# Attention B: the values of a pair of heads weighed on 64 output columns each, in plain float32

## The reference, cut to what matters

```python
def swa_mixer(h, w_in, b_in, sinks, w_out, b_out, rel_bias):
    ...
    kk, vv = with_prev(k), with_prev(v)
    logits = jnp.einsum('bnqkgd,bnskd->bnkgqs', q, kk).astype(jnp.float32) * (Dh ** -0.5)
    ...
    p = jax.nn.softmax(jnp.concatenate([logits, sink], axis=-1), axis=-1)[..., :-1]
    o = jnp.einsum('bnkgqs,bnskd->bnqkgd', p.astype(vv.dtype), vv)
    return o.reshape(B, T, N_HEADS * Dh) @ w_out + b_out
```

## Time and profile before

| | before |
|---|---|
| median of 3 runs | 1174.75 us (1174.5 to 1175.15) |
| profiled execution, device time | 1174.45 us |
| its span, first to last instruction | 1172.7 us |
| PE busy | 1153.3 us |
| PEld busy | 962.8 us |
| POOL busy | 610.4 us |
| DVE busy | 529.9 us |
| ACT busy | 458.0 us |
| granted TensorE clock, mean | 0.998 |

### The profile page before, as it was taken

The page is one execution under the profiler, slowest core; times in us unless marked ns, Lnnn a source line. Parts: engine busy times, 40 slices in busy tenths (PEclk is TensorE's granted clock), DMA queues, the critical chain, the costliest instruction groups (busy, mean ns, idle before and its releaser), DMA issues.

```text
span 1172.7 us, 16085 instructions
## 1 busy us (share of the span) xinstructions
PE 1153.3 (98%) x5666; PEld 962.8 (82%) x5666; DVE 529.9 (45%) x931; ACT 458.0 (39%) x854; POOL 610.4 (52%) x359
## 2 busy tenths in 40 slices
PE   7999999999999999999999999999999999999997
PEld 5778889888888888888888888888888888888887
DVE  5479967743543443441111376645444434420001
ACT  5343267754333223223222477643322332322333
POOL 5427667864454454444444587834445544534441
PEclk9999999999999999999999999999999999999999
DMA  7442311123323323323443332322333333232331
GB/s 241 151 136 72 126 37 46 46 72 108 104 76 107 107 77 102 107 75 106 142 129 102 102 86 57 66 70 74 108 107 89 89 107 99 68 90 88 94 98 72
DMA packets 181572, 112.46 MB, mean 96 GB/s; under 512 B 7340, under 2 KB 175591, under 8 KB 181528
## 3 DMA queue, kind: packets, MB, share of 16 engines
q1 hardware_dynamic: 180860, 110.71, 31.7%
q10 hardware_dynamic: 668, 1.19, 0.3%
HBM read 109.72 MB, written 8.45 MB: 101 GB/s over the span
## 4 chain that ended last, share of the span: by engine, by line
PE 93%; DVE 3%; issue 1%; ACT 1%; POOL 1%; DMA 1%; ACTq 0%; DVEq 0%
PE ps L607 29%; PE ps L609 29%; PE ps L608 29%; PE ps L616 1%; PE ps L842 1%; DVE work L1639 1%; PE ps L1021 1%; PE ps L816 1%; DMA x_tok<-in_x 1%; DVE work L1621 0%; PE ps L1024 0%; POOL w_lo L494 0%; POOL work L554 0%; PE ps L655 0%; DVE xs_lo L1524 0%
## 5 line engine op out<-in xcount | busy, mean ns | idle before, releaser
L494 POOL TENSOR_TENSOR w_lo<-raw,w_hi 128x1024 fp32r<-128x1024 f32 (+1 forms) x198 | 454.1, 2316 | 479.7 <-ACT w_hi L1147 471.1
L607 PE MATMUL ps<-xs_hi,w_hi 128*128 128x512 f32 (+3 forms) x1024 | 397.2, 388 | 4.0 <-POOL w_lo L494 1.6
L608 PE MATMUL ps<-xs_lo,w_hi 128*128 128x512 f32 (+3 forms) x1024 | 394.4, 385 | 0.0
L609 PE MATMUL ps<-xs_hi,w_lo 128*128 128x512 f32 (+3 forms) x1024 | 394.3, 385 | 0.0
L1147 ACT CAST w_hi<-raw 128x1024 fp32r<-128x1024 f32 (+1 forms) x194 | 177.1, 962 | 430.3 <-PE ps L609 430.3
L607 PEld LDWEIGHTS ps<-xs_hi,w_hi 128*128 128x128 f32 x1024 | 192.2, 188 | 47.4 <-issue 4.1
L608 PEld LDWEIGHTS ps<-xs_lo,w_hi 128*128 128x128 f32 x1024 | 192.3, 188 | 39.1 <-issue 1.0
L609 PEld LDWEIGHTS ps<-xs_hi,w_lo 128*128 128x128 f32 x1024 | 192.3, 188 | 38.5
L607 PE MATMUL ps<-act_hi,w_hi 128*128 128x512 f32 (+1 forms) x374 | 141.6, 379 | 0.0
L609 PE MATMUL ps<-act_hi,w_lo 128*128 128x512 f32 (+1 forms) x374 | 140.9, 377 | 0.0
L608 PE MATMUL ps<-act_lo,w_hi 128*128 128x512 f32 (+1 forms) x374 | 140.8, 377 | 0.0
(11 more groups left out here) (191 smaller groups left out, 1348.0 us busy)
## 6 DMA issues: line engine op xcount, KB each, us to landing
raw<-in_ffn_w_gate_up SPq DMA_DIRECT2D x88, 512.0 KB, 4.3
raw<-in_ffn_w_down SPq DMA_DIRECT2D x32, 384.0 KB, 3.4
raw<-in_a_w_in SPq DMA_DIRECT2D x20, 512.0 KB, 4.8
raw<-in_ffn_w_down SPq DMA_DIRECT2D x32, 320.0 KB, 3.9
bias_toep<-bias_row SPq DMA_DIRECT2D x4, 1024.0 KB
toep<-bias_toep SPq DMA_DIRECT2D x16, 256.0 KB, 2.6
raw<-in_a_w_out SPq DMA_DIRECT2D x8, 512.0 KB, 4.3
raw<-in_b_w_in SPq DMA_DIRECT2D x8, 512.0 KB, 5.0
```

What stands on the lines that cost most here:

```text
L494: nc.gpsimd.tensor_tensor(pieces(w_lo, n)[half], pieces(raw, n)[half], pieces(w_hi, n)[half].bitcast(F32), ALU.subtract)\
L607: nc.tensor.matmul(dst, wh, xh, start=start, stop=False, **kw)
L608: nc.tensor.matmul(dst, wh, xl, start=False, stop=False, **kw)
L609: return nc.tensor.matmul(dst, wl, xh, start=False, stop=stop, **kw)
```

## The change

`b_weigh` no longer uses `mm3`. The values are kept whole in one float32 tile `b_v` without padding, the turned probabilities in one float32 tile `bpt`. Head a uses 64 weight columns, `b_v[:, s, r[a]]`, and writes to 64 partitions of bank 7. Per pair there are 8 matmuls: for each block s one of a = 0 and one of a = 1. The turned probabilities leave PSUM once, bank 5 by a copy on ACT (`b_turned_fore`), bank 6 by a copy on DVE (`b_turned_rear`). The values leave PSUM by one copy on ACT. POOL's two memsets of the padding, DVE's remainders of the values and of the turned probabilities, and the casts in between are gone.

```diff
-            pool.wait_ge(unit_done, U_BK)
-            nc.gpsimd.memset(v_hi[:, :, :, :].bitcast(F32), 0.0).then_inc(pad_done, 1)
-            nc.gpsimd.memset(v_lo[:, :, :, :].bitcast(F32), 0.0).then_inc(pad_done, 1)
...
@@ b_turn
-                        pe.wait_ge(bptl_done, 4 * h2 + 2 * a - 1 + b)
+                        pe.wait_ge(bpt_copied[b], 2 * h2 + a)
...
@@ b_weigh
-                for a in range(2):
-                    for s in range(NB):
-                        if s % 2 == 0:
-
-                            pe.wait_ge(bptl_done, 4 * h + 2 * a + s // 2 + 1)
...
-                        last = mm3(ps[:, 7, s * P:s * P + n], v_hi[:, a, s, :], v_lo[:, a, s, :],
-                                   bpt_hi[:, h % 2, a, s * 2 * P:s * 2 * P + n],
-                                   bpt_lo[:, h % 2, a, s * 2 * P:s * 2 * P + n],
-                                   a == 0 and s == 0, a == 1 and s == NB - 1, skip_group_check=True)
+                r = (slice(0, DH), slice(DH, P))
+                for s in range(NB):
+                    if s % 2 == 0:
+
+                        pe.wait_ge(bpt_copied[s // 2], 2 * h + 2)
+                    n = 2 * P if s < NB - 1 else P
+                    for a in range(2):
+                        last = nc.tensor.matmul(ps[r[a], 7, s * P:s * P + n], b_v[:, s, r[a]],
+                                                bpt[:, h % 2, a, s * 2 * P:s * 2 * P + n],
+                                                start=s == 0, stop=s == NB - 1, skip_group_check=True)
...
@@ ACT
-            act.wait_ge(pad_done, 2)
-            for a in range(2):
-                nc.scalar.copy(v_hi[:, a, :, a * DH:(a + 1) * DH],
...
+            nc.scalar.copy(b_v[:, :, :], ps[:, 7, :].rearrange("p (s c) -> p s c", s=NB)).then_inc(v_done, 1)
...
+            def b_turned_fore(h, a):
+
+                act.wait_ge(bpt_done, 4 * h + 2 * a + 1)
...
+                nc.scalar.copy(bpt[:, h % 2, a, 0:4 * P], ps[:, 5, :]).then_inc(bpt_copied[0], 1)
...
@@ DVE
+            def b_turned_rear(h, a):
+
+                dve.wait_ge(bpt_done, 4 * h + 2 * a + 2)
...
+                nc.vector.tensor_copy(bpt[:, h % 2, a, 4 * P:WIN], ps[:, 6, 0:3 * P]).then_inc(bpt_copied[1], 1)
```

More of the change, by code:

```diff
@@ L203, in trunk @@
         bk_lo = sb("bk_lo", [P, T], F32R, bmem)
-        v_hi = sb("v_hi", [P, 2, NB, P], F32R, bmem)
-        v_lo = sb("v_lo", [P, 2, NB, P], F32R, bmem)
+        b_v = sb("b_v", [P, NB, P], F32, bmem)
         b_prob = sb("b_prob", [P, 2, 2, WIN], F32, bmem)
@@ L211, in trunk @@
         kv_m.close()
-        bpt_hi = sb("bpt_hi", [P, 2, 2, WIN], F32R, bmem)
-        bpt_lo = sb("bpt_lo", [P, 2, 2, WIN], F32R, bmem)
+        bpt = sb("bpt", [P, 2, 2, WIN], F32, bmem)
         bmem.close()
@@ L282, in trunk @@
             sem(n) for n in ("gate_done", "up_done", "silu_done", "glu_done", "ah_done", "al_done"))
-        kvr_done, kvb_done, bkh_done, bkl_done, v_tr, vh_done, vl_done, pad_done = (
-            sem(n) for n in ("kvr_done", "kvb_done", "bkh_done", "bkl_done", "v_tr", "vh_done", "vl_done", "pad_done"))
+        kvr_done, kvb_done, bkh_done, bkl_done, v_tr, v_done = (
+            sem(n) for n in ("kvr_done", "kvb_done", "bkh_done", "bkl_done", "v_tr", "v_done"))
         sink_done, nqb_done, bqr_done = sem("sink_done"), sem("nqb_done"), sem("bqr_done")
@@ L290, in trunk @@
         bnrm_done = [sem("bnrm_done0"), sem("bnrm_done1")]
-        bpt_done, bpth_done, bptl_done, bo_done, boh_done, bol_done = (
-            sem(n) for n in ("bpt_done", "bpth_done", "bptl_done", "bo_done", "boh_done", "bol_done"))
+        bpt_done, bo_done, boh_done, bol_done = (sem(n) for n in ("bpt_done", "bo_done", "boh_done", "bol_done"))
+        bpt_copied = [sem("bpt_copied_act"), sem("bpt_copied_dve")]
         y_done, y_tr, y_copied, out_done = sem("y_done"), sem("y_tr"), sem("y_copied"), sem("out_done")
@@ L1036, in b_weigh @@
                     pe.wait_ge(bol_done, h)
-                for a in range(2):
-                    for s in range(NB):
-                        if s % 2 == 0:
-                            pe.wait_ge(bptl_done, 4 * h + 2 * a + s // 2 + 1)
-                        if a == 0 and s == 0 and h == 0:
-                            pe.wait_ge(vl_done, 2)
-                        n = 2 * P if s < NB - 1 else P
-                        last = mm3(ps[:, 7, s * P:s * P + n], v_hi[:, a, s, :], v_lo[:, a, s, :],
-                                   bpt_hi[:, h % 2, a, s * 2 * P:s * 2 * P + n],
-                                   bpt_lo[:, h % 2, a, s * 2 * P:s * 2 * P + n],
-                                   a == 0 and s == 0, a == 1 and s == NB - 1, skip_group_check=True)
+                if h == 0:
+                    pe.wait_ge(v_done, 1)
+                r = (slice(0, DH), slice(DH, P))
[7 more added lines that the diff above has]
+                                                start=s == 0, stop=s == NB - 1, skip_group_check=True)
                 last.then_inc(bo_done, 1)
@@ L1427, in _ @@
             act.wait_ge(v_tr, 1)
-            act.wait_ge(pad_done, 2)
-            for a in range(2):
-                nc.scalar.copy(v_hi[:, a, :, a * DH:(a + 1) * DH],
-                               ps[:, 7, :].rearrange("p (s c) -> p s c", s=NB)[:, :, a * DH:(a + 1) * DH])\
-                    .then_inc(vh_done, 1)
+            nc.scalar.copy(b_v[:, :, :], ps[:, 7, :].rearrange("p (s c) -> p s c", s=NB)).then_inc(v_done, 1)
             act.wait_ge(sink_in, 16)
@@ L1438, in b_heads_hi @@
                 nc.scalar.copy(bo_hi[:, h, :], ps[:, 7, :]).then_inc(boh_done, 1)
[L1440 to L1447, removed]
+            def b_turned_fore(h, a):
+                act.wait_ge(bpt_done, 4 * h + 2 * a + 1)
+                if h >= 2:
+                    act.wait_ge(bo_done, h - 1)
+                nc.scalar.copy(bpt[:, h % 2, a, 0:4 * P], ps[:, 5, :]).then_inc(bpt_copied[0], 1)
             def b_exponents(k, a):
@@ L1465, in _ @@
                 if k >= 2:
-                    b_turned_hi(k - 2, 0)
+                    b_turned_fore(k - 2, 0)
                 if 1 <= k < DM - 1:
@@ L1470, in _ @@
                 if k >= 2:
-                    b_turned_hi(k - 2, 1)
+                    b_turned_fore(k - 2, 1)
                 if k >= 3:
@@ L1475, in _ @@
             for h in (DM - 2, DM - 1):
-                b_turned_hi(h, 0)
-                b_turned_hi(h, 1)
+                b_turned_fore(h, 0)
+                b_turned_fore(h, 1)
                 b_heads_hi(h - 1)
@@ L1830, in _ @@
             b_q_part(1)
[L1832 to L1836, removed]
             def b_heads_lo(h):
@@ L1852, in b_invert @@
                 nc.vector.reciprocal(b_rinv[:, par, :, :].rearrange("p a i -> p (a i)"), sums).then_inc(brinv_done, 1)
[L1854 to L1861, removed]
+            def b_turned_rear(h, a):
+                dve.wait_ge(bpt_done, 4 * h + 2 * a + 2)
+                if h >= 2:
+                    dve.wait_ge(bo_done, h - 1)
+                nc.vector.tensor_copy(bpt[:, h % 2, a, 4 * P:WIN], ps[:, 6, 0:3 * P]).then_inc(bpt_copied[1], 1)
             def b_lowest(k, a):
@@ L1886, in _ @@
                 if k >= 2:
-                    b_turned_lo(k - 2, 0)
+                    b_turned_rear(k - 2, 0)
                 if 1 <= k < DM - 1:
@@ L1891, in _ @@
                 if k >= 2:
-                    b_turned_lo(k - 2, 1)
+                    b_turned_rear(k - 2, 1)
                 if k >= 3:
@@ L1896, in _ @@
             for h in (DM - 2, DM - 1):
-                b_turned_lo(h, 0)
-                b_turned_lo(h, 1)
+                b_turned_rear(h, 0)
+                b_turned_rear(h, 1)
                 b_heads_lo(h - 1)
```

## The result

| | before | changed |
|---|---|---|
| median of 4 runs | 1174.73 us | 1167.23 us (1166.84 to 1167.32) |
| profiled execution, device time | 1174.45 us | 1167.31 us |
| its span | 1172.7 us | 1165.5 us |

The ratio is 0.9936, with a 95% interval of 0.9924 to 0.9947: 7.5 us faster. The forecast was 1169.0, with a range of 1167.3 to 1174.6; the median lies 0.07 us under its lower end.

What follows compares the result with a forecast made beforehand. PE bounds the kernel (98% busy). Gains of 2.16 us (passes 3 to 5), 1.15 (passes 6 and 7) and 2.16 (weighings 5 to 7), together 5.5, take 1174.45 to 1168.95; forecast median 1169.0 us, range 1167.3 to 1174.6.

Steps and rivals of the forecast that it cites:

- passes 6 and 7: Attention B up to the first turn of pair 6: two weighings save 1.44 us, of which 1.15 is kept because of POOL.
- the rest: Weighings 5 to 7 of attention B, where everything behind is PE after PE: 2.16 us gained.
- one correction: In each weighing, head 0's record 2 overlaps only head 1's record 1: a 0.22 us lag, 1.73 us instead of 1.51.
- Going in and out of halves: Change of form at both ends of each weighing, read from the logits on row halves: 0.31 us, paid once per weighing.
- How much sooner POOL comes: First turn of pair 6: POOL's stretch starts up to 0.4 us sooner through DVE's inverse; 1.15 us taken, 0.95 without it.
- The other parts: New copies (0.5 us each), memsets and value work: hidden behind PE, gaining nothing; the next turn still finds DVE's copy done.
- edges of nothing: Low end of the full side-by-side case: a weighing takes 1.73 us, gaining 7 to 8 us less what POOL gives back.
- the likeliest case: Weighing with both column halves fully side by side, the forecast itself: own range 1167.3 to 1170.5 us, chance 0.55.
- One after the other: Rival: column halves do not overlap, a weighing takes 3.34 us, 0.58 more; 1178.0 us, chance 0.18.
- loads exposed: Rival: no weights fetched during a matmul of the same rows, a weighing takes 4.2 us; about 1185 us, chance 0.02.
- The hitch: Rival: side by side, but 0.055 to 0.11 us lost at each change of half; 1172.2 to 1175.3 us, chance 0.20.
- Other helpers too slow: Rival: the other engines, POOL above all, bound the shorter passes and half the gain goes; 1171.8 us, chance 0.05.

Runs made afterwards that it cites:

- the first experiment: Changed kernel with values zero-padded so each plain float32 matmul takes the whole array instead of a column half: 1175.98 us, ratio 1.001 to the kernel before.
- the head-by-head kernel: Changed kernel with the two loops of `b_weigh` swapped, four matmuls of head 0 and then four of head 1: 1173.63 us, ratio 0.999 to the kernel before.
- The kernel with half of POOL's split left out: Changed kernel with the second half of POOL's weight-slab split between pairs 5 and 6 cut to 8 of 1024 columns, given to nobody: 1166.83 us.
- the split in turn: Changed kernel with DVE splitting the second half of the weight slab between pairs 5 and 6 first, POOL the first half afterwards: 1166.53 us.
- The copies alone: Kernel before with only the way out of PSUM changed to one ACT and one DVE copy, 24 float32r matmuls kept: 1174.11 us, ratio 0.9996.
- the kernel with one head: Changed kernel without head 1 of each pair in the weighing, four matmuls instead of eight on the first column half: 1167.23 us.
- the first shared kernel: Changed kernel with DVE taking the second half of POOL's weight-slab split between pairs 5 and 6, without waiting in turn: 1167.58 us.

## Why the prediction was wrong

The sign, the mechanism and the place were right: plain float32 costs 3.03 us on the whole array, as the first experiment shows to the hundredth, and the halves buy it back. The size was wrong. The forecast took 5.5 us off; the traces, with the changed kernel's 0.39 us of lateness before pass 3 taken out, show where 7.5 came from:

| stretch | forecast | from the two traces |
|---|---|---|
| passes 3 to 5 | 2.16 | 2.98 (logits of pair 6: 730.46 before, 727.87 now) |
| passes 6 and 7 | 1.15 | 1.61 (piece behind the first turn of pair 6: 748.47, 744.27) |
| the rest | 2.16 | 2.94 (last matmuls of the kernel 7.14 apart) |

- **The step that failed** is the "one correction" under "Second, whether they do": that record 2 of head 0 can only overlap with record 1 of head 1, a lag of 0.22 us. It was argued from an order of starts that no row showed. The windows at 701.40 show two starts at once; the head-by-head kernel shows a half starting three records ahead of its turn. Without the lag a weighing is 1.51 + 0.31 = 1.82 us, measured 1.81. The six weighings outside passes 6 and 7 make 1.6 of the 2.1 us that were missed.
- **Going in and out of halves**, taken from the logits on row halves at 0.31 us, was right: 1.81 - 1.51 = 0.30.
- **How much sooner POOL comes** is the second term that was too small. That POOL would be next late at the first turn of pair 6 was right. The text bounded passes 6 and 7 by it, 0.95 us and what POOL comes sooner by itself, and took 0.2 for that. POOL's scalings of pair 6 start at 740.60, where they started at 743.83 before: 3.23 + 0.39 - 2.98 = 0.64 us sooner than the shorter passes 3 to 5 make them. 0.95 + 0.64 = 1.59, measured 1.61. Most of the 0.64 is DVE, which gives POOL its inverse for 729.08 instead of 732.20.
- **What lies behind POOL.** The kernel with half of POOL's split left out gains 0.2 to 0.4 us, not the 1.0 that PE's two waits summed to, because DVE's copy was done only 0.56 us before the second of them ended. Part of DVE's lateness is the hold by POOL: in that kernel the sum still ends only with POOL's first subtraction, at 738.45, and the wait of 0.30 us in pass 7 stands; in the split in turn neither is there, and PE no longer waits for DVE's copy at pair 6.
- **The other parts** were not all free. The text held that the next turn still finds DVE's copy done. That is so in passes 3 to 5; in pass 7 PE waits 0.30 us for it. The split in turn shows that the wait goes when DVE's sum is not held up. The copies alone gave 0.6 us, within the uncertainty. A reading was wrong too: POOL idles 2 us or more in pass 5 but not in pass 4, where the trace of the kernel before has it busy 9.94 of 11.60 us; nothing hung on it.
- **The range.** That the median lies only 0.07 us under its end is no merit of the sum. Its lower end stands for "edges of nothing", and the edges were 0.30. The value without the lag, 1.51 us and edges, stood in the text too, as what the Trainium skill's rule would make (page TensorEngine Tiling (Array Packing), section Key Properties: different tiles can run weight loads and matmuls in parallel; the trace agrees, with two starts at 701.40). It was kept from the sum, since no row showed column halves, but no case and no chance were given to it. By the text's own terms it would have made 6 x 0.94 + 1.15 = 6.8 us, or 1168.0 for the median; the rest is POOL. The upper end of the likeliest case, 1170.5, does not follow from the text either: edges twice as large, with a gain of 3.4 us, make 1171.4.
- **The rivals.** One after the other, and loads exposed: excluded by the kernel with one head, which takes as long as the one with two. The hitch: the changed kernel's 16 records fill 1.66 us with no room for it. Other helpers too slow: passes 3 to 5 have no gap on PE; the one late copy costs 0.30 us in pass 7.

## What to carry to other kernels

When a product fills only half of the array's columns, try its partner beside it on the other half: here the second one cost nothing, and that paid for a number format that is dearer per matmul. Interleave the two in program order; one after the other, 6.4 of the 7.5 us were lost. Whether three float32r matmuls on halves would be faster still, no run here shows. And when a limit is found in the profile, look at what stands 0.5 us behind it before pricing its removal: here relief of POOL led straight to DVE, which POOL itself had held up.

## What the runs showed of the hardware that was not expected

Matmuls on two column halves do not start in program order. A first record on the second half started in the same instant as one of the first half that stood two records ahead, and in the head-by-head kernel 0.91 us after the first start, with three records of the other half still ahead of it.

The same subtraction of 128x1024 from and to SBUF took DVE 1.22 us alone and 2.89 us while POOL did one of its own. In the second case POOL's instruction ran from 735.44 to 737.82, and DVE's ended at 738.90, 1.08 us later: most of what it takes alone came after POOL was through. POOL's took 2.38 us in both. The short sum shows it more sharply, because it needs next to no time itself: 0.16 to 0.17 us alone, and in the changed kernel 1.71 us from 736.60 on, to 0.03 us behind the end of POOL's subtraction. It was so in the kernel before too (0.89 us from 740.62 on, to 0.02 us behind POOL's end). The Trainium skill says so (page SBUF — State Buffer, section SBUF: two separate sides, on the shared port pair: whichever of a DVE instruction with two SBUF inputs and a GpSimd instruction that reads SBUF starts first holds the pair for the whole instruction, and the other blocks). The trace agrees where POOL subtracts, and the expectation of the first shared kernel missed it. Where POOL scales, which also reads SBUF, the trace shows no such hold: DVE's next sum starts and ends within one scaling.

```profile
743.89 0.61 POOL L585 TENSOR_SCALAR b_prob<-b_prob,b_rinv 128x128 f32<-128x128 f32 x1
744.10 0.17 DVE L1834 TENSOR_TENSOR b_rsum<-b_rsum,b_sinkp 128x8 f32<-128x8 f32 x1
```
